# A two-block transformer kernel on one core: the recurrence tiles' 64-token chunk inverse as 32x32 blocks, 64-column key products, a fused state update, and the tile loop written out

## The reference

```python
def wkv_scan(r, v, decay, k, a_in, b_in, s0, reverse):
    def step(S, inp):
        rt, vt, wt, kt, at, bt = inp
        sa = jnp.einsum('bhij,bhj->bhi', S, at)
        S = S * wt[:, :, None, :] + sa[..., None] * bt[:, :, None, :] + vt[..., None] * kt[:, :, None, :]
        return S, jnp.einsum('bhij,bhj->bhi', S, rt)
    xs = tuple(jnp.moveaxis(z, 1, 0) for z in (r, v, decay, k, a_in, b_in))
    s_end, ys = lax.scan(step, s0, xs, reverse=reverse)
    return jnp.moveaxis(ys, 0, 1), s_end
```

## Time and profile before

| | |
|---|---|
| three runs | 4441.8, 4454.0, 4456.9 us; median 4454.0 |
| the profiled execution | 4448.1 us; its span 4446.4 us |
| mean granted TensorE clock | 0.962 |
| busy share of the span | PE 94%, PE weight load 66%, DVE 29%, ACT 16%, POOL 6% |
| instructions | 51,347, of them 21,570 MATMUL |
| chain that ended last | PE 88%, DVE 6%, DMA 3%, issue 2%, ACT 1% |

### The profile page before, as it was taken

How to read it: one execution, slowest core, us unless ns; L and a number is a source line. 1 busy time by engine, 2 the same in 40 slices (tenths; PEclk the granted TensorE clock), 3 DMA queues, 4 the chain that set the end, 5 groups by cost and what they waited for, 6 DMA issues and landing times.

```text
span 4446.4 us, 51347 instructions
## 1 busy us (share of the span) xinstructions
PE 4171.1 (94%) x21570; PEld 2930.6 (66%) x21570; DVE 1290.2 (29%) x2777; ACT 728.6 (16%) x1553; POOL 288.6 (6%) x326
## 2 busy tenths in 40 slices
PE   5999999999999998899999999988988988899998
PEld 3447545544446676776776857776775777788887
DVE  1000344620023222130034135555455555100001
ACT  2100122310011221120022012222222222000000
POOL 0000000000000003100000001210220122000000
PEclk9999999999999999999999999989999978799999
DMA  8433322233434336853212420011001000344443
GB/s 342 163 136 129 114 95 95 86 153 140 151 112 155 136 119 158 230 209 133 76 59 105 147 84 21 20 40 40 21 20 40 31 1 1 104 143 160 152 158 126
DMA packets 77504, 489.58 MB, mean 110 GB/s; under 512 B 10480, under 2 KB 14576, under 8 KB 23648
## 3 DMA queue, kind: packets, MB, share of 16 engines
q1 hardware_dynamic: 70560, 462.45, 29.0%
q0 software_dynamic: 6720, 23.78, 2.0%
HBM read 482.00 MB, written 4.19 MB: 109 GB/s over the span
## 4 chain that ended last, share of the span: by engine, by line
PE 88%; DVE 6%; DMA 3%; issue 2%; ACT 1%; POOL 0%; DVEq 0%; ACTq 0%; POOLq 0%
PE ps L930 47%; PE ps L1031 7%; PE ps L924 7%; PE ps L1137 3%; PE ps L1122 3%; PE ps L869 3%; PE ps L990 3%; PE ps L1134 3%; PE ps L1009 2%; PE ps L927 2%; DMA w<-in_wi 1%; PE ps L1000 1%; PE ps L1162 1%; DVE zone L2023 1%; PE ps L1174 1%
## 5 line engine op out<-in xcount | busy, mean ns | idle before, releaser
L930 PE MATMUL ps<-h,w 128*128 128x256 f32 (+1 forms) x4992 | 1554.4, 463 | 51.7 <-DMA w<-in_wi 34.6
L930 PEld LDWEIGHTS ps<-h,w 128*128 128x128 f32 x4992 | 940.4, 193 | 509.2 <-issue 409.8
L930 PE MATMUL ps<-y,w 128*128 128x256 f32 (+1 forms) x1792 | 507.8, 441 | 1.7 <-DMA w<-in_wo 1.7
L930 PEld LDWEIGHTS ps<-y,w 128*128 128x128 f32 x1792 | 338.0, 190 | 156.4 <-issue 121.9
L1031 PE MATMUL ps<-h,w 128*128 128x256 f32 (+1 forms) x1024 | 370.3, 501 | 1.3 <-issue 1.3
L924 PE MATMUL ps<-w,h 128*128 128x256 f32 x1280 | 278.6, 379 | 0.0
L924 PEld LDWEIGHTS ps<-w,h 128*128 128x128 f32 x1280 | 243.0, 190 | 38.5 <-issue 6.1
L1031 PEld LDWEIGHTS ps<-h,w 128*128 128x128 f32 x1024 | 182.2, 189 | 111.8 <-issue 91.3
L817 POOL TENSOR_TENSOR zone<-zone 128x512 f32<-128x512 f32 x160 | 203.1, 1272 | 641.5 <-DVE zone L2019 352.7
L869 PE MATMUL ps<-w,zone 128*32 128x256 f32 x2304 | 150.0, 403 | 25.3 <-DVE zone L2083 11.7
L1137 PE MATMUL ps<-zone 128*128 128x128 f32 x1280 | 168.3, 275 | 0.0
(11 more groups left out here) (306 smaller groups left out, 3887.0 us busy)
## 6 DMA issues: line engine op xcount, KB each, us to landing
w<-in_wm SPq DMA_DIRECT2D x144, 1024.0 KB, 8.0
w<-in_we SPq DMA_DIRECT2D x52, 1024.0 KB, 5.0
w<-in_w SPq DMA_DIRECT2D x48, 1024.0 KB, 5.0
w<-in_wmg SPq DMA_DIRECT2D x48, 1024.0 KB, 5.0
w<-in_wi SPq DMA_DIRECT2D x34, 1024.0 KB, 5.1
w<-in_wo SPq DMA_DIRECT2D x32, 1024.0 KB, 5.0
w<-in_wrw SPq DMA_DIRECT2D x32, 1024.0 KB, 5.0
w<-in_wbr SPq DMA_DIRECT2D x48, 512.0 KB, 4.3
```

Of the source, the lines that this page charges most:

```text
L930: last = mm(pass_psum(s, q), rows[:, n * P:(n + 1) * P], src[k], start=(k == 0), stop=(k == s.kt - 1))
```

## The change

Outside the recurrence tiles nothing is touched. Inside them:

1. The products for the inverse are made as 32x32 blocks (`rw_blocks`, 128 matmuls for a tile, both the matrix and its transpose, so the transposes of it go away), the off-diagonal 32x32 corners apart (`rw_corners`, 32), and the other key products as 64x64 chunks (`rw_keys`, `rw_reads`, 64).
2. The inverse of a 64x64 chunk becomes two 32x32 diagonal blocks by four levels of doubling, and one corner product (`o21`, `zs`, 64 matmuls). A block of 32 tokens sits in its own 32 partitions, so that matmuls with 32 rows and 32 columns go to four array positions in turn.
3. In the recurrence the two directions share one accumulator of 128 columns for `w1` and `us_` (two before), next step's own-chunk products are issued early (`rw_own`), the latent outputs add up in one PSUM bank over the steps and are copied once, and the state update reads PSUM directly: two instructions where three stood in a chain of two.
4. The projections are handed out over inverse and recurrence, one matmul at a time.
5. The loops over tiles are written out on all engines; the POOL engine scales the factors by the last chunk's decay (`fas`, `frs`).

Matmuls of the program for one tile, without the 64 of the projection: 456 before, 1268 now. Of the 1268, 992 have 32x32 outputs (blocks, corners, doubling, corner product), 232 have 64x64.

The core of the diff:

```diff
+            def rw_blocks(it):
+                for x in range(2):
+                    for tok in range(4):
+                        for d in range(2):
+                            for g in range(4):
+                                for hd in range(2):
+                                    c = slice(tok * P + 32 * g, tok * P + 32 * g + 32)
+                                    b, a = fbk[half_rows(hd), 0, d, c], far[half_rows(hd), d, 0, c]
+                                    at = x * 256 + tok * 64 + d * 32
+                                    last = mm(ps[quarter(g), 3 + hd, at:at + 32], b if x == 0 else a, a if x == 0 else b,
+                                              start=True, stop=True)
...
+                for l in range(4):
+                    for p in range(2):
+                        pe.wait_ge(s_am, 4 * it + l + 1)
...
+                        for tok in (2 * p, 2 * p + 1):
+                            for i in range(4):
+                                for g in range(4):
+                                    r, at = quarter(g), (tok % 2) * P + i * 32
+                                    last = mm(ps[r, 3 + 2 * p, at:at + 32], am[r, l, tok, i // 2, i % 2, :],
+                                              xx[r, 1, tok, i // 2, i % 2, :], start=True, stop=True)
+                        last.then_inc(s_pp, 1)
...
+                    for p in range(2):
+                        pe.wait_ge(s_pe, 8 * it + 2 * l + p + 1)
+                        for x in range(2):
+                            for tok in (2 * p, 2 * p + 1):
+                                for i in range(4):
+                                    for g in range(4):
+                                        r, at = quarter(g), (tok % 2) * P + i * 32
+                                        mine = pb[r, p, tok % 2, i, :]
+                                        xt = xx[r, 0, tok, i // 2, i % 2, :]
+                                        last = mm(ps[r, 4 + 2 * p, x * 256 + at:x * 256 + at + 32], xt if x else mine,
+                                                  mine if x else xt, start=True, stop=True)
+                        last.then_inc(s_dt, 1)
...
+                    pe.wait_ge(s_w1e, 8 * it + i + 1)
+                    for hd in range(2):
+                        for d, (tok, hf) in enumerate(ds):
+                            r = half_rows(hf)
+                            last = mm(ps[r, 5, P + 64 * hd:P + 64 * hd + 64], xt64[r, tok, hd, d, :, :], w1[r, half_rows(hd)],
+                                      start=True, stop=True)
+                    last.then_inc(s_u, 1)
+                    if i < 7:
+                        rw_own(i + 1, False)
...
-            with pe.Fori(1, 6) as it:
-                rw_invert(it)
-                rw_recur(it, rw_features(it + 1), rw_project(it + 2))
+            for it in range(8):
+                rw_invert(it, rw_passes(it + 1, (2, 3)) if it < 7 else iter(()))
+                rw_recur(it, rw_passes(it + 2, (0, 1)) if it < 6 else iter(()), it + 1 if it < 7 else None)
```

On DVE, the inverse and the state update (the first lines are one unit of the inverse before, 20 units for a tile; 8 now):

```diff
-                for k in range(20):
-                    tok = k % 4
-                    wait(s_dt, 20, k + 1)
-                    if k < 16:
-                        v = tn[:, tok, :, :].rearrange("p a t -> p (a t)")
-                        v_.tensor_tensor(v, v, ps[:, 4 + k % 2, :], ALU.add)
-                    v = xt[:, tok, :, :].rearrange("p a t -> p (a t)")
-                    v_.tensor_tensor(v, v, ps[:, 6 + k % 2, :], ALU.add).then_inc(s_te, 1)
...
+                def update(l, p):
+                    dve.wait_ge(s_dt, 8 * it + 2 * l + p + 1)
+                    v = xx[:, :, 2 * p:2 * p + 2, :, :, :].rearrange("p x k h d t -> p x (k h d t)")
+                    v_.tensor_tensor(v, v, ps[:, 4 + 2 * p, :].rearrange("p (x t) -> p x t", x=2), ALU.add).then_inc(s_te, 1)
...
-                        step(v_.tensor_tensor(state, state, ps[:, 5:7, 0:P], ALU.add))
-                        for d, (tok, hf) in enumerate(ds):
-                            c = 2 * tok + hf
-                            last = v_.scalar_tensor_tensor(state[:, d, :], state[:, d, :], dtot_s[:, d, c:c + 1],
-                                                           head_ones, ALU.mult, ALU.mult)
+                        for d, (tok, hf) in enumerate(steps(i - 1)):
+                            c = 2 * tok + hf
+                            last = v_.scalar_tensor_tensor(state[:, d, :], state[:, d, :], dtot[:, it % 2, d, c:c + 1],
+                                                           ps[:, 5 + d, 0:P], ALU.mult, ALU.add)
```

More of the change, by code:

```diff
@@ L1141, in rw_recur @@
[L1141 to L1154 removed]
+                mm(ps[:, 2, 0:NL], head_ones, yq, start=True, stop=True).then_inc(s_ssq2, 1)
@@ new lines, in rw_corners @@
+            def rw_corners(it, hd):
+                for tok in range(4):
+                    for d in range(2):
+                        for hf in range(2):
+                            c = tok * P + 64 * hf
+                            first, second = slice(c + 32 * d, c + 32 * d + 32), slice(c + 32 - 32 * d, c + 64 - 32 * d)
+                            last = mm(ps[quarter(2 * hf + d), 2 if hd else 7, tok * 32:tok * 32 + 32],
+                                      fbk[half_rows(hd), 0, d, first], far[half_rows(hd), d, 0, second], start=True, stop=True)
+                last.then_inc(s_cor, 1)
@@ new lines, in rw_own, with rw_out_state @@
+            def rw_own(i, last_start):
+                for d, (tok, hf) in enumerate(steps(i)):
+                    r = half_rows(hf)
+                    for hd in range(2):
+                        last = mm(ps[r, 7, 64 * hd:64 * hd + 64], mak[r, tok, hd, d, :], btk[r, 0, tok, half_rows(hd)],
+                                  start=(hd == 0), stop=last_start, skip_group_check=True)
+                return last
+            def rw_out_state(i, d, first):
+                tok, hf = steps(i)[d]
+                c0 = (tok - 2) * P + 64 * hf
+                for hd in range(2):
+                    mm(ps[half_rows(hd), 4, c0:c0 + 64], state[:, d, half_rows(hd)], frs[:, d, c0:c0 + 64],
+                       start=first, stop=False, skip_group_check=True)
@@ new lines, in rw_recur @@
+                        if i == 1:
+                            pe.wait_ge(s_fold, it + 1)
+                        for d, (tok, hf) in enumerate(ds):
+                            last = mm(ps[half_rows(hf), 7, 0:P], fas[:, d, tok * P + 64 * hf:tok * P + 64 * hf + 64],
+                                      state[:, d, :], start=False, stop=True, skip_group_check=True)
+                        last.then_inc(s_w1, 1)
+                    if i >= 4:
+                        for d in range(2):
+                            rw_out_state(i, d, i == 4 and d == 0)
```

964 lines of the change are left out of this document (541 added, 423 removed).

## The result

The changed kernel takes 4256.7 us in the median of four runs (4248.4 to 4261.5), against 4453.1 us for the kernel before in four. The ratio is 0.9563, with a 95% interval of 0.9547 to 0.9579: 196 us faster. The forecast was 4245 us.

A forecast was written before the change was run, and what follows sets the result against it. TensorE's own work was taken to bound tiles 0 to 5, with a chain of waits in the recurrence of 6 and 7. Terms -126 - 38 - 13 - 32 = -209 us gave 4245 us; the forecast's own range was 4160 to 4350.

The forecast's parts named there:

- A tile with projections: One tile's inverse and recurrence: -66.3 + 29.8 + 3.7 + 8 + 9 = -15.8 us, eight times -126.
- the price of a 32-column matmul: 992 matmuls a tile, two instructions each: 30 ns a matmul between ends of 15 and 58, 29.8 us a tile.
- the sentence on issue: Upper end for 32-column matmuls: 29 ns an instruction, 58 ns a matmul, if issuing and not the array sets the pace.
- rival 4: 32-column matmuls: all four positions at once, fed in time; 15 ns a matmul, 4150 us; chance 13%.
- Rival 1: Issue-bound: TensorE's sequencer feeds one pair of weight load and matmul every 29 ns at best; 58 ns a matmul, 4467 us; 10%.
- 4 us more of waits and no change of its small work: Recurrence of a tile: some 0.5 us more waits a step, 4 us; 18 smaller matmuls in place of 14, zero.
- Waits of the inverse: Inverse of a tile: 3 us at the start, 2 us at the end, 2 us for corner product and recurrence start.
- Loop, -38: Tile starts in the loop: four jumps at 9.5 us go away, -38 us.
- Ahead of tile 0, -13: Projections and features before tile 0: 52.1 us become 36 to 40 with 32 projection matmuls in place of 64; -13.
- Tiles 6 and 7, -31.8 each: Last two tiles, nothing over their chain: recurrence steps some 3 us instead of 4.4; -32 us beyond the -15.8 a tile.
- Rival 2: Doubling: matmuls of four row positions into one PSUM bank go one after another; 62 ns a matmul, 4499 us; 15%.
- Rival 3: Inverse at half clock, 32x32 work counting as little: over 50 us more a tile, 4650 us; 5%.

The follow-up runs named there:

- e4: Changed kernel with doubling operands (L1204, L1230) read as bfloat16, one instruction pair in place of two, lower precision: 4084.4 us, ratio 0.9178.
- e5: Changed kernel with the transposed 32x32 blocks made by VectorE in place of matmuls, same result: 4085.5 us, ratio 0.9181.
- e7: Changed kernel with the own-chunk products (L1274) of a recurrence step put back behind the wait for the state: 4271.9 us, ratio 0.9599.
- e1: Kernel before with its tile loops written out on all engines, nothing else changed: 4419.2 us, ratio 0.9928.
- e3: Changed kernel with the loop over the four array positions outermost in L1204 and L1230, same instructions in other order: 4616.2 us, ratio 1.0367.

## Why the prediction came out right, and where it did not

- **Total.** 4245 forecast, 4256.7 measured. The profiled execution fell by 4446.4 - 4257.8 = 188.6 us where the sum said 209.
- **A tile with projections.** The sum said -15.8 us; tile 5 went from 145.8 to 129.9. This agreement is two errors that cancel. By the prediction's own terms the inverse should go from 70.7 to about 65 with its 13.8 us of projections (-66.3 + 29.8 + 3.7 + 8 + 5 of waits + 13.8) and the recurrence lose 9.8 (-13.8 + 4). Measured: inverse +3.2, recurrence -19.1.
- **The step that failed** is the price of a 32-column matmul, and with it the sentence on issue. I asked only at what pace the engine starts instructions, one by one. The groups start them every 8.6 ns at full clock, rival 4's pace and its sign, faster than I took; yet the price is 43 ns a matmul (drains in it) and not 15, since the instructions themselves do not arrive. e4 and e5 show it: 3.7 and 4.0 us for a piece of 128 pairs. Rival 1 had the size of a piece (29 ns a pair) with the wrong mechanism: TensorE does not start pairs evenly 29 ns apart, it runs at 8.6 ns and then stops at the end of a piece. Its 4467 us did not come, since part of each 3.7 us lies under wide matmuls.
- **The other error** is in the recurrence, for which 4 us more of waits and no change of its small work were forecast. The stretch of tile 5's recurrence now is below: TensorE is busy 55.9 of 56.0 us, and its small work fell by 5.3 us (75.1 less 41.3 of projections before, 56.0 less 27.5 now), where I wrote zero. Which part of the new recurrence gives the 5.3 us no run shows; e7 took back the early own products, and tiles 0 to 5 lost nothing by it.

```profile
3360.50:3416.50 56.00, 55.92 (x441) 25.97 (x441) 27.13 (x56) 11.26 (x25) 0.00 (x0) 0.93 0.07 21
```

- **Waits of the inverse** for other engines: 2.89 us for DVE at its start, as forecast (3), but 0.88, 0.48 and 0.42 at its end, 1.8 us together where 2 + 2 were forecast. The first of them in the timeline:

```profile
3300.51 1.07 PE L1204 MATMUL ps<-zone 32*32 32x32 f32 x64 [2.89 <-DVE zone L2239]
```

- **Loop, -38.** 38.8 us in e1's trace. Tiles 1 to 4 of the changed kernel save 102 us, forecast 101.
- **Ahead of tile 0, -13.** 94.1 us became 76.2, -17.9.
- **Tiles 6 and 7, -31.8 each.** They gave 24.1 and 22.6. The chain's part held (tile 7's recurrence 52.4 to 34.5 us; steps of 3.6 us in place of 4.4 and more, the answer to the earlier trace rows). Tile 7's inverse gave 4.8 us in place of 20: 2145 pairs are 17 pieces, at 3.7 us 62 of its 65.8 us, with no projections in them. Its stretch, and two steps of its recurrence:

```profile
3531.60:3597.40 65.80, 43.66 (x2145) 38.65 (x2144) 17.11 (x27) 11.60 (x24) 9.67 (x12) 0.58 0.02 4
```

```profile
3604.55 0.69 PE L1316 MATMUL ps<-y,x_latent 128*64 128x128 f32 x4 [0.73 <-DVE y L2281]
...
3608.14 0.70 PE L1316 MATMUL ps<-y,x_latent 128*64 128x128 f32 x4 [0.73 <-DVE y L2281]
```

- **Outside.** +7 us: tile 0's first projection starts at 2562.3 where it started at 2555.5. That work is the same, and its start lay between 2554.1 and 2576.9 in the experiments' profiles, e1 with the old tiles at 2562.6; it is the spread of single executions.
- **Rival 2**, one bank at a time, is refuted: 8.6 ns from four row positions into one bank. One position at a time they come every 27 to 29.5 ns (e3). The rule of the Trainium skill, page "TensorEngine Tiling (Array Packing)", Gotcha 1, does not show here.
- **Rival 3**, half clock, happened in part. The forecast said 1.00 in tiles 0 to 5; it is 0.87 and 0.88. It seems to have cost little where the pieces, not the array, set the time; e3 shows what it costs where the array does.

## What to carry to other kernels

Count instructions as well as columns. Where TensorE would run through 128 pairs of weight load and matmul in less than 3.7 us, they arrived too late here, and the cure was fewer instructions (transposes on VectorE, -171 us) before any finer packing; wide matmuls spread between small ones took in part of the wait. And when a sum comes out right, compare its terms by part: this one was right with the inverse 9 us too good and the recurrence 9 us too bad.

## What the runs showed of the hardware that I had not expected

- Instructions came in pieces of 16,384 bytes, mostly 3.5 to 4.0 us apart when TensorE wanted them faster and no weight panel moved, each with 0.9 to 1.5 us of transfer; in tile 5 TensorE stopped after 128 pairs or a multiple. The waits were longer, up to 4.7 us, while a weight panel's transfer was moving.
- At a stop TensorE went on 1.2 to 1.6 us after the piece's transfer had ended, and the next piece's transfer began 1.05 us or more after that.
- Four row and column positions with 32x32 weights start a pair every 8.6 ns at full clock and every 13.3 at half, into one PSUM bank; one position every 27 to 29.5 ns at full clock, 45 to 49 at half.
- VectorE transposes eight 32x32 blocks in each of its four groups of 32 partitions (128x256 float32) in 0.45 us, about what it takes for an addition of that size (0.42).
- What fills the two pauses around a transfer, 1.1 and 1.4 us, is open; no run here changed them.
